# A hybrid decoder layer on one core: two weight places swapped, three weight loads and the overflow list moved in program order

## What is computed

```python
xn   = rms_norm(x, norm_mix_w)
proj = xn @ w_in                       # 1024 x 3072: b, c, h, q, k, v
# 8 channel groups: y_c = b * causal_conv3(c * h);  8 heads of 64: stick-breaking attention
x = x + concat([norm(y_c), norm(y_a)]) @ w_out
xn2  = rms_norm(x, norm_ffn_w)
g    = argmax(xn2 @ w_group + b_group)             # 1 of 4 groups
e    = top_k(experts of group g, 2)                # 2 of 8 experts
gate = p_g * softmax(top_v)
# every (token, choice) pair goes to its expert, 32 experts in all:
h = silu(xb @ w1[e]) * (xb @ w3[e])                # w1, w3: 1024 x 512
y = h @ w2[e]                                      # w2: 512 x 1024
x = x + sum over the two choices of gate * y
```

## Time and profile before

| | us |
|---|---|
| median of 3 runs | 1163.53 |
| lowest, highest | 1162.94, 1165.76 |
| the profiled execution | 1164.72 |
| its span | 1163.0 |
| TensorE busy | 1099.6 (95%) |
| VectorE busy | 904.1 (78%) |
| ScalarE busy | 717.6 (62%) |
| GpSimd busy | 135.3 (12%) |

### The profile page before, as it was taken

One profiled execution on the slowest core, in us unless ns is written; L12 is line 12 of the kernel. 1 busy time (PEld: TensorE's weight loads), 2 busy tenths in 40 slices (PEclk: granted clock), 3 DMA queues, 4 the chain that ended last, 5 costly groups with the idle time before them and its releaser, 6 DMA issues. The chain is left out here.

```text
span 1163.0 us, 16827 instructions
## 1 busy us (share of the span) xinstructions
PE 1099.6 (95%) x5770; PEld 899.0 (77%) x5770; DVE 904.1 (78%) x1048; ACT 717.6 (62%) x882; POOL 135.3 (12%) x194
## 2 busy tenths in 40 slices
PE   8999999999999899999999999999999999999950
PEld 7887777778777668888778888888888888888840
DVE  5405957678575772578989999999999999999947
ACT  5423555646643571133678888888888888888830
POOL 1001000000000120011011110110111111101000
PEclk9999999999999999998999999999999999999985
DMA  7111232313213353004999999999999999999519
GB/s 235 42 36 38 92 88 61 104 39 107 67 46 95 108 214 136 37 37 175 387 427 426 397 390 393 387 387 392 381 383 388 384 390 379 385 382 385 212 74 378
DMA packets 77118, 275.22 MB, mean 237 GB/s; under 512 B 20771, under 2 KB 51619, under 8 KB 63888
## 3 DMA queue, kind: packets, MB, share of 16 engines
q1 hardware_dynamic: 66272, 253.69, 57.3%
q0 software_dynamic: 9216, 16.72, 3.8%
q10 hardware_dynamic: 1584, 4.20, 0.9%
HBM read 259.57 MB, written 31.85 MB: 251 GB/s over the span
## 5 line engine op out<-in xcount | busy, mean ns | idle before, releaser
L1211 DVE TENSOR_TENSOR e_lo<-W,e_hi 128x1024 fp32r<-128x1024 f32 x384 | 452.5, 1220 | 25.2 <-ACT e_hi L1205 22.3
L1205 ACT ACTIVATE e_hi<-W 128x1024 fp32r<-128x1024 f32 x384 | 402.5, 1059 | 99.6 <-PE ps L1176 87.6
L1174 PE MATMUL ps<-e_hi,xT_hi 128*128 128x512 f32 x496 | 197.6, 398 | 1.9 <-DVE e_lo L1211 1.9
L1176 PE MATMUL ps<-e_lo,xT_hi 128*128 128x512 f32 x496 | 194.9, 393 | 0.0
L1175 PE MATMUL ps<-e_hi,xT_lo 128*128 128x512 f32 x496 | 194.3, 392 | 0.0
L472 PE MATMUL ps<-xnT_hi,w_hi 128*128 128x512 f32 x320 | 129.1, 404 | 1.6 <-DVE u L861 0.7
L472 PE MATMUL ps<-xnT_hi,w_lo 128*128 128x512 f32 x320 | 128.0, 400 | 0.0
L472 PE MATMUL ps<-xnT_lo,w_hi 128*128 128x512 f32 x320 | 125.4, 392 | 0.0
L900 DVE TENSOR_TENSOR_SCAN kept<-kept,start_at 128x1024 f32<-128x1024 f32 (+7 forms) x64 | 88.4, 1381 | 28.5 <-ACT kept L702 28.4
L1174 PEld LDWEIGHTS ps<-e_hi,xT_hi 128*128 128x128 f32 x496 | 94.2, 190 | 20.4 <-issue 2.0
L1176 PEld LDWEIGHTS ps<-e_lo,xT_hi 128*128 128x128 f32 x496 | 93.8, 189 | 20.1
(11 more groups left out here) (256 smaller groups left out, 1687.4 us busy)
## 6 DMA issues: line engine op xcount, KB each, us to landing
W<-in_w_dram SPq DMA_DIRECT2D x96, 2048.0 KB, 13.4
w_raw<-in_w_in_dram SPq DMA_DIRECT2D x20, 512.0 KB, 4.1
yy<-y_rows SPq DMA_DIRECT2D x7, 1024.0 KB, 12.1
xt<-in_x_dram SPq DMA_DIRECT2D x8, 512.0 KB, 3.9
w_out_raw<-in_w_out_dram SPq DMA_DIRECT2D x8, 512.0 KB, 6.4
xn_rows<-xn SPq DMA_DIRECT2D x8, 512.0 KB, 2.9
out_dram<-x ACTq DMA_DIRECT2D x7, 512.0 KB, 8.7
x<-in_x_dram SPq DMA_DIRECT2D x2, 1536.0 KB, 10.6
```

The lines of the kernel that those rows point to most:

```text
L1174: pe.matmul(o, xs_hi[:, k], hi[:, p, cols], start=(k == 0), stop=False)
L1176: mm = pe.matmul(o, xs_hi[:, k], lo[:, p, cols], start=False, stop=(k == last))
L1205: act.activation(hi[:, p], flat[:, p * D:(p + 1) * D], ACT.Copy).then_inc(s["hi_made"], 1)
L1211: dve.tensor_tensor(lo[:, p], flat[:, p * D:(p + 1) * D], hi[:, p], ALU.subtract).then_inc(s["lo_made"], 1)
```

## The change

It has four parts. The places of W2 are swapped, so that W2 of expert 0 lies at 48 KB and W2 of expert 1 on the router's tables. On SP, W3 of expert 1 no longer waits for the gather of expert 1's rows, W2 of expert 0 follows it with no wait, then come W1 and W3 of expert 2; the wait for the list stands only before W2 of expert 1, behind them. On TensorE expert 1's rows are turned after two pieces of expert 0's up product instead of three, the column is turned into the list in round 1 (into bank 7, where nothing is written afterwards), and nothing waits for `over_ready`. On VectorE `pick_blocks` comes behind all four pieces of W1 of expert 1, and `list_blocks` and `make_gates` behind the last split of the last expert.

```diff
--- before.py
+++ after.py
@@ -142,7 +142,7 @@
 
         W1 = [at(f"W1_{i}", kib, [P, KT, F]) for i, kib in enumerate((112, 16))]
         W3 = [at(f"W3_{i}", kib, [P, KT, F]) for i, kib in enumerate((0, 32))]
-        W2 = [at(f"W2_{i}", kib, [P, FT, D]) for i, kib in enumerate((96, 48))]
+        W2 = [at(f"W2_{i}", kib, [P, FT, D]) for i, kib in enumerate((48, 96))]
 
         small = [int(196.5 * KIB)]
 
@@ -1046,7 +1046,7 @@
         NOH = 4
         HOTS = 2 * NT
         RANK_AT = ((3, 0), (1, 0), (3, 0), (6, 2 * P))
-        TABLE, FIRST_AT, COUNT_AT, LIST_AT = 7, (3, P), (4, 0), (6, 3 * P)
+        TABLE, FIRST_AT, COUNT_AT, LIST_AT = 7, (3, P), (4, 0), (7, 3 * P)
         iota = place("iota", [P, COLS])
         iota_p1 = place("iota_p1", [P, 1])
         iota_pick = place("iota_pick", [P, EPG])
@@ -1347,22 +1347,21 @@
                     sp.wait_ge(xn2_made, m + 1 if m < NT - 1 else NT + 1)
                     sp.dma_start(xn2_rows_v[m], xn2[m % 2]).then_inc(xn2_stored[m % 2], 16)
                 sp.dma_start(W1[1], w1_v[1]).then_inc(expert_w[1][0], 16)
-                sp.wait_ge(s_e["gathered"][1], 16)
                 sp.dma_start(W3[1], w3_v[1]).then_inc(expert_w[1][1], 16)
+                sp.dma_start(W2[0], w2_v[0]).then_inc(expert_w[0][2], 16)
+
+                def load(w, wv, e, b, landed, n):
+
+                    sp.wait_ge(s_e["lo_made"], n + PIECES)
+                    sp.dma_start(w[b], wv[bass.ds(e, 1)].rearrange("e p k f -> p (e k) f")).then_inc(expert_w[b][landed], 16)
+
+
+                sp.wait_ge(s_e["freed"], used(gate_start(0) + PIECES))
+                load(W1, w1_v, 2, 0, 0, gate_start(0))
+                load(W3, w3_v, 2, 0, 1, up_start(0))
                 sp.wait_ge(listed, 1)
                 sp.wait_ge(list_turned, 1)
-                sp.dma_start(W2[0], w2_v[0]).then_inc(expert_w[0][2], 16)
-
-                def load(w, wv, e, b, landed, n):
-
-                    sp.wait_ge(s_e["lo_made"], n + PIECES)
-                    sp.dma_start(w[b], wv[bass.ds(e, 1)].rearrange("e p k f -> p (e k) f")).then_inc(expert_w[b][landed], 16)
-
-
-                sp.wait_ge(s_e["freed"], used(gate_start(0) + PIECES))
-                load(W1, w1_v, 2, 0, 0, gate_start(0))
                 sp.dma_start(W2[1], w2_v[1]).then_inc(expert_w[1][2], 16)
-                load(W3, w3_v, 2, 0, 1, up_start(0))
                 with sp.Fori(1, NE // 2 - 1) as i:
                     for b in (1, 0):
                         e = 2 * i + 2 - b
@@ -1618,13 +1617,12 @@
                     if not (isinstance(e, int) and e == 0):
                         pe_turn_hid(pe, s_e, e - 1)
                     else:
-                        pe_product(pe, s_e, up_start(0), xT_hi, xT_lo, [ps[:, 3]], 2, KT - 1, (0, 1, 2))
+                        pe_product(pe, s_e, up_start(0), xT_hi, xT_lo, [ps[:, 3]], 2, KT - 1, (0, 1))
                         pe_turn_x(pe, s_e, 1, 1, 1)
-                        pe_product(pe, s_e, up_start(0), xT_hi, xT_lo, [ps[:, 3]], 2, KT - 1, (3,))
-                        overflow_list()
+                        pe_product(pe, s_e, up_start(0), xT_hi, xT_lo, [ps[:, 3]], 2, KT - 1, (2, 3))
                         return
                     if isinstance(e, int) and e == 1:
-                        pe.wait_ge(over_ready, 1)
+                        overflow_list()
                     pe_up(pe, s_e, e, up_start(e))
                     if not last and not (isinstance(e, int) and e == 0):
                         pe_turn_x(pe, s_e, e + 1, 1 - b, rounds + b)
@@ -2006,14 +2004,11 @@
                         dve_split(dve, s_e, gate_start(e), W1[b])
                     if isinstance(e, int) and e == 0:
                         dve_split(dve, s_e, up_start(0), W3[0])
+                        dve_split(dve, s_e, gate_start(1), W1[1], (0, 1))
+                        dve_xT(dve, s_e, 1)
+                        dve_split(dve, s_e, gate_start(1), W1[1], (2, 3))
                         pick_blocks()
-                        dve_split(dve, s_e, gate_start(1), W1[1], (0,))
-                        dve_xT(dve, s_e, 1)
-                        dve_split(dve, s_e, gate_start(1), W1[1], (1,))
-                        list_blocks()
-                        make_gates()
                         dve_hid(dve, s_e, 0, up_start(0))
-                        dve_split(dve, s_e, gate_start(1), W1[1], (2, 3))
                         return
                     dve_split(dve, s_e, up_start(e), W3[b])
                     if not (isinstance(e, int) and e == 0):
@@ -2038,6 +2033,8 @@
                 dve_split(dve, s_e, down_start(NE - 1), W2[1], (0, 1))
                 dve_hidT(dve, s_e, NE - 1)
                 dve_split(dve, s_e, down_start(NE - 1), W2[1], (2, 3))
+                list_blocks()
+                make_gates()
 
 
                 def over_body(n):
```

More of the change, by code:

```diff
@@ L1349, in _ @@
                 sp.dma_start(W1[1], w1_v[1]).then_inc(expert_w[1][0], 16)
-                sp.wait_ge(s_e["gathered"][1], 16)
                 sp.dma_start(W3[1], w3_v[1]).then_inc(expert_w[1][1], 16)
-                sp.wait_ge(listed, 1)
-                sp.wait_ge(list_turned, 1)
                 sp.dma_start(W2[0], w2_v[0]).then_inc(expert_w[0][2], 16)
@@ L1363, in _ @@
                 load(W1, w1_v, 2, 0, 0, gate_start(0))
+                load(W3, w3_v, 2, 0, 1, up_start(0))
+                sp.wait_ge(listed, 1)
+                sp.wait_ge(list_turned, 1)
                 sp.dma_start(W2[1], w2_v[1]).then_inc(expert_w[1][2], 16)
-                load(W3, w3_v, 2, 0, 1, up_start(0))
                 with sp.Fori(1, NE // 2 - 1) as i:
```

## The result

| | before | after |
|---|---|---|
| median of the runs | 1163.12 us (1162.00 to 1166.33, 9 runs) | 1167.27 us (1166.19 to 1170.16, 9 runs) |
| ratio, 95% interval | | 1.0034 (1.0023 to 1.0044) |
| profiled execution | 1164.72 us, span 1163.0 | 1167.91 us, span 1166.2 |

The change makes the kernel 4.15 us slower where I forecast +0.9: inside my range, but the interval excludes my value (1.0007), and it lies just outside the 3.5 us that I had called no change.

What follows compares the result with a forecast made beforehand. The loop was taken as bound by TensorE, so only its ends could change: -7.1 taken away, +7.8 for the gather's stop and clock, +0.2 tail = +0.9 us, 1164.4 us against 1163.53; range 1159 to 1169.

Steps and rivals of the forecast that it cites:

- the case "slower": Whole kernel: slower by over 0.3% (3.5 us), chance 0.21.
- What the change takes away: Passage from router to expert 2: TensorE's waits and restarts, 5.4 us, plus 1.7 of low clock, gone: 7.1 us.
- All three waits: TensorE: 0.67 ahead of and 2.07 inside expert 1's gate product, 1.88 us ahead of expert 2's up product; all go.
- the clock at 587: Expert 2's up product: clock granted at 0.58 for 587 to 591 us, costing 1.7 us, which the change removes.
- W2 of expert 1, late next: After the change this transfer waits for the list; its lateness was priced at nothing, covered by products of 5.44 us.
- The gather: Expert 1's rows, asked for at 548.96 us, meet a full queue: 11.0 us, landing at 559.96.
- The stop: TensorE at the transposes of expert 1's rows: 6.1 us idle plus 1.7 of low clock, 7.8 us added.
- the sign of expert 2's up product: TensorE: this product should end within a microsecond of 594.15 us.
- The tail: End of kernel: SP's later walk over overflow blocks ends in a dead heat with the last scatter: +0.2 us.
- The gather slips through: Rival: expert 1's gather lands near 555.4, TensorE stops 1.5 us and keeps its clock: 1158.1 us, chance 0.15.
- As long as in the loop: Rival: expert 1's gather takes 14.9 us, landing at 563.86, and TensorE stops 10.0 us: 1168.3 us, chance 0.2.
- The change frees nothing: Rival: SP still stands before W3 of expert 1, only VectorE's 2.3 us wait goes: 1161.4 us, chance 0.03.

Runs made afterwards that it cites:

- after_again: The changed kernel itself, run again beside the kernel before: 1166.91 us, ratio 1.0032.
- wait_before_w2: Changed kernel with SP's wait for expert 1's gather put back between W3 of expert 1 and W2 of expert 0: 1159.03 us, again 1159.42 us.
- list_only: Kernel before with only the list (in bank 7) and the gates moved behind the last split: 1165.91 us, ratio 1.0016.
- loads_only: Changed kernel with the gather wait ahead of W3 of expert 1; list, gates, block picking and TensorE's pieces as before the change: 1162.10 us.
- wait_back: Changed kernel with SP's wait for expert 1's gather put back ahead of W3 of expert 1: 1160.89 us, ratio 0.9968.
- wait_behind_w2: Changed kernel with SP's wait for expert 1's gather put back behind W2 of expert 0: 1163.77 us, ratio 1.0001.
- list_early: Changed kernel with the list made ahead of the last expert's round, gates still at the end: 1167.03 us, ratio 1.0025.

## Why the prediction was right, and where its sizes were off

The path was right: the gather takes its place on the chain and TensorE stops for it. The forecast of no change was not: by my own edge of 3.5 us the 4.15 are the case "slower", to which I gave 0.21. The range was wide enough to hold the best kernel here as well (1159.0), so that it held this one says little.

- **What the change takes away: 7.1 us.** Right, in this profile. The change needs 596.80 - 554.31 = 42.5 us for the work that took 594.15 - 553.99 = 40.2; less its 9.2 us of wait and low clock, 33.3 are left, so 6.9 went. All three waits are gone, and in 620 to 1100 us nothing new came. But 1.7 of it was the clock at 587, and the traces show that a stop of that size does not always bring it (last section). A median may never have held it in full. That could be why the medians differ by 4.15 and the two profiles by 3.2; it was not tested.
- **W2 of expert 1, late next, at nothing.** Right. SP waited 19.4 us for the list's matmul at 573.13, and ScalarE never waited for a weight transfer afterwards.
- **The gather: 11.0 us.** The mechanism was right, the size short. 12.1 (11.2 in `after_again`), and its issue came 0.3 us later, so rows landed at 561.4 where I had 559.96. The row that I took it from the earlier trace rows was of the same kind, a gather amid weights, and nearly all of the 1.1 us lies in the issue instruction. The timeline of GpSimd in the kernel before:

```profile
557.57 1.01 POOL L1257 DMA_INDIRECT xg<-xn_rows,idx_token  x1 [0.85 <-POOL idx_token L1253]
```

  Behind that instruction the gather took 11.0 - 1.0 = 10.0 us there, 12.12 - 1.97 = 10.15 in the change and 11.20 - 1.24 = 9.96 in `after_again`. So what the queue costs was forecast to 0.2 us; the issue of 1.97 us was not.
- **The stop: 6.1 us + 1.7 of clock.** 7.1 + 2.1. With 6.9 taken away and 0.3 of lateness from ahead of 554 the front is +2.65 us, not +0.7, and the sign of expert 2's up product (within a microsecond of 594.15) failed. This is the term that was mis-sized: 1.4 of the 2.3 us that the profile is off. The rest is 0.2 and 0.3 in the front and 0.6 behind the first sum, less 0.3 in the tail. That a stop brings the low clock I had from the row at 587; the row at 563.86, a stop of 2.07 us behind which the clock stayed at 1.00, speaks against it for short stops, and I passed it over.
- **The tail: +0.2 us.** -0.07, and near by luck: two errors cancel. The walk ended at 1131.1 as computed, moved by the front; but the scatter took 3.2 us, not the 4.2 of the earlier trace rows, so the walk was 0.9 us late and no dead heat. Both together give what the tail had before.
- **The rivals.** *The gather slips through* is refuted for a full queue, and is what happens with one transfer ahead: 5.3 us, and the 1158.1 us that I gave it against the 1159.0 of `wait_before_w2`. *As long as in the loop* did not happen to expert 1's rows (it needed a landing behind 562.6), though the second gather, issued at 552.4, took 15.1 us. *The change frees nothing* is refuted: all three waits went. Its price, 2.3 us for VectorE's wait alone, would not have come either: `list_only` took that wait away and gained nothing.

## What to carry to other kernels

A wait that seems to idle a queue can be what keeps a small, urgent transfer fast. Before taking it away, list what is needed first behind it (here the rows at 554, W3 of expert 1 at 560, W2 much later) and let ahead only what would itself be late: one transfer let ahead made it 4.5 us faster than before, no wait at all 4 us slower. When a small transfer meets a queue of large packets, a first estimate is its packets per engine, each at a turn with one large packet (0.66 to 0.75 us here), and what the engines already hold (3.1 to 3.3 us to its first packet here, 0.6 with an empty queue). When one stall hides another, removing one alone can show nothing, as the list did here: test the pair.

## What the runs showed that I had not expected

**The last scatter takes 3.2 or 4.2 us, and a packet of instructions goes with the longer one.** It took 4.1 to 4.2 us in the kernel before and in `loads_only`, and 3.2 in the ten profiles of the other kernels. The DMA queues of the kernel before, 1125 to 1129 us:

```profile
q0 software_dynamic: 144, 0.26, 17.0%
q14 instruction: 1, 0.01, 1.1%
```

and of the changed one, 1128 to 1130 us:

```profile
q0 software_dynamic: 144, 0.26, 33.8%
```

The 144 packets are the scatter. In the two kernels with 4.1 to 4.2 us a packet of instructions falls among them: 0.011 x 16 x 4 = 0.7 us on one of the 16 engines. None does in the others. The rates tell how the scatter ends (GB/s, one value per 0.15 us), in the kernel before for 1124 to 1130 us and in the changed one for 1126.5 to 1132.5:

```profile
GB/s 0 0 0 55 0 0 0 0 0 0 0 0 192 247 191 191 191 218 191 218 27 27 27 27 27 27 0 0 0 0 0 0 0 0 0 0 55 273 0 109
...
GB/s 0 0 0 0 0 55 0 0 0 0 0 0 0 219 220 218 218 218 218 191 218 27 0 0 0 0 0 0 0 0 0 0 0 0 0 0 0 437 328 0
```

27 GB/s for 0.15 us is one packet of 4 KB. Before, the scatter ends in six such values, with the change in one: for some 0.75 us one packet runs at a time, as if a single engine were late by the 0.7 us of the instruction packet. Both kernels with the longer scatter have the list in expert 0's round, so their code is laid out otherwise. That the packet is the cause fits size and place, but no run moved it.

**A stop of 2 us brought the low clock in two cases of six; the four longer ones here did each time.** After stops of 1.88 us (the kernel before at 587, granted 0.58) and 2.02 (`wait_back`, 0.66 for 567 to 572) it fell. After stops of 2.07 (the kernel before at 563.86 and `loads_only`) and of 1.83 and 2.27 (`list_only`) it stayed at 1.00, that is 2.4 GHz. After the stops of 3.51 (`wait_behind_w2`), 6.05 (`after_again`), 6.45 (`list_early`) and 6.96 us (the change) it was 0.50, that is 1.2 GHz, for the matmuls that followed. The long waits of `wait_back` and of `loads_only`, alike in length, therefore cost 3.7 and 2.1 us in their profiles (expert 1's up product takes 7.15 us in the one, 1.7 over the 5.44 of full clock). The row of `wait_back`'s windows behind its wait:

```profile
567.00:572.00 5.00, 4.52 (x13) 3.60 (x14) 4.96 (x7) 3.45 (x5) 0.00 (x0) 0.66 1.03 441
```

and that of `loads_only`:

```profile
565.00:570.00 5.00, 4.93 (x23) 4.17 (x24) 5.00 (x6) 4.51 (x5) 0.00 (x0) 1.00 1.03 435
```

The twelve runs of `wait_back` fall into two groups, six from 1158.2 to 1159.9 us and six from 1161.9 to 1163.9, and its median of 1160.89 lies in the gap between them; the profile is one of the upper six. The low clock after its wait may be what parts them, but no run of the lower group was profiled, and `loads_only` has two groups as well (1160.2 to 1161.0 and 1162.1 to 1163.1), with its profile in the upper one at full clock behind its wait. The cause is open. It means that `wait_back` is behind `wait_before_w2` by its upper group: its lower one is as fast.
